# Eight rows of V sent for before the sixteenth row of U, a last V row moved from VectorE to TensorE, and a store that no longer waits, in a one-layer diffusion backbone with a PEER expert stage

## The reference, cut to what matters

```
q  = hx @ w_q                                  # per head two halves of 128
v1, i1 = top_k(q1 @ k1.T, 16); v2, i2 = top_k(q2 @ k2.T, 16)
score, pos = top_k(v1[:, None] + v2[None, :], 16);  idx = (i1 * 128 + i2)[pos]
gate = softmax(score)
act  = gelu(sum_d w_u[idx] * hx)               # 16 dot products of 2048
out += sum_k (gate * act)[k] * w_v[idx[k]]     # 16 rows of 2048
```

## Time and profile before

| | |
|---|---|
| median of 3 runs | 3055.89 us (3055.28 to 3056.6) |
| the profiled execution's own time | 3055.89 us |
| its span in the trace | 3054.1 us |
| PE, DVE, ACT, POOL busy | 87%, 63%, 30%, 20% of the span |
| DMA | 902.85 MB, 296 GB/s over the span |
| gathers of U and V | 256 and 256, of 1 MB each |

### The profile page before, as it was taken

The page is one execution under the profiler, slowest core; times in us unless marked ns, Lnnn a source line. Parts: engine busy times, 40 slices in busy tenths (PEclk is TensorE's granted clock), DMA queues, the critical chain, the costliest instruction groups (busy, mean ns, idle before and its releaser), DMA issues.

```text
span 3054.1 us, 31614 instructions
## 1 busy us (share of the span) xinstructions
PE 2652.6 (87%) x11033; PEld 1802.4 (59%) x11033; DVE 1931.8 (63%) x2623; ACT 911.5 (30%) x1240; POOL 607.3 (20%) x580
## 2 busy tenths in 40 slices
PE   8899997999998999999999956969778876868777
PEld 3488875878776879999878723434333432323332
DVE  1389997444555868888556675555555565656656
ACT  1067765442444333333444110101111111101100
POOL 0000000000000000000000174434344435443333
PEclk9999998999999999999999988989989998989999
DMA  8533333552422877888556699999999999999999
GB/s 337 220 124 124 110 109 127 193 190 85 152 83 112 337 307 304 334 339 316 193 207 237 247 420 409 422 421 412 421 412 421 403 422 411 421 403 421 421 422 376
DMA packets 126508, 902.85 MB, mean 296 GB/s; under 512 B 14016, under 2 KB 15552, under 8 KB 17216
## 3 DMA queue, kind: packets, MB, share of 16 engines
q0 software_dynamic: 82944, 604.02, 48.0%
q1 hardware_dynamic: 38736, 278.94, 24.4%
q10 hardware_dynamic: 4720, 18.57, 1.6%
HBM read 899.33 MB, written 2.13 MB: 295 GB/s over the span
## 4 chain that ended last, share of the span: by engine, by line
PE 44%; DMA 28%; DVE 13%; issue 9%; ACT 3%; POOL 2%; DVEq 0%; ACTq 0%; POOLq 0%
DMA u<-in_peer_u,idx 26%; PE ps L446 9%; PE ps L489 8%; PE ps L490 7%; PE ps L491 7%; PE ps L766 5%; PE ps L504 3%; DVE u L1671 2%; DVE wl L1149 2%; DMA v<-in_peer_v,idx 2%; POOL u L1756 1%; POOL v L1766 1%; ACT wh L828 1%; DVE ub L1233 1%; PE ps L643 1%
## 5 line engine op out<-in xcount | busy, mean ns | idle before, releaser
L766 PE MATMUL ps<-v,dg 128*128 128x512 f32 x1920 | 878.4, 614 | 178.0 <-DMA v<-in_peer_v,idx 101.8
L1671 DVE SCALAR_TENSOR_TENSOR u<-u,hN 128x2048 f32<-128x2048 f32 x256 | 586.4, 2291 | 470.8 <-DMA u<-in_peer_u,idx 459.6
L1149 DVE TENSOR_TENSOR wl<-w,wh 128x1024 fp32r<-128x1024 f32 x432 | 524.4, 1221 | 408.8 <-ACT wh L828 407.8
L766 PEld LDWEIGHTS ps<-v,dg 128*128 128x128 f32 x1920 | 368.3, 196 | 683.9 <-issue 512.4
L828 ACT ACTIVATE wh<-w 128x1024 fp32r<-128x1024 f32 x432 | 453.5, 1058 | 679.2 <-PE ps L491 411.9
L1756 POOL DMA_INDIRECT u<-in_peer_u,idx x256 | 279.3, 1091 | 846.1 <-DVE u L1671 447.3
L446 PE MATMUL ps<-both,wh 128*128 128x256 f32 x2048 | 372.3, 285 | 5.2 <-DVE y L1361 5.1
L1101 ACT ACTIVATE dg<-con,wt 128x128 f32<-128x128 f32 x240 | 93.1, 399 | 836.6 <-PE ps L766 832.1
L1766 POOL DMA_INDIRECT v<-in_peer_v,idx x256 | 293.9, 1148 | 175.0 <-PE ps L766 89.2
L446 PEld LDWEIGHTS ps<-both,wh 128*128 128x128 f32 x2048 | 320.9, 193 | 10.1 <-issue 8.9
L1748 POOL DMA_DIRECT2D mr<-in_wmod x64 | 34.0, 532 | 1399.6 <-DVE br_lo L1489 980.5
(11 more groups left out here) (240 smaller groups left out, 2803.4 us busy)
## 6 DMA issues: line engine op xcount, KB each, us to landing
w<-in_stream SPq DMA_DIRECT2D x260, 1024.0 KB, 4.8
mr<-in_wmod POOLq DMA_DIRECT2D x64, 1024.0 KB, 6.8
wg<-in_gates ACTq DMA_DIRECT2D x8, 512.0 KB, 3.5
wx<-in_stream SPq DMA_DIRECT2D x4, 1024.0 KB, 7.8
u<-in_peer_u,idx POOLq DMA_INDIRECT x256, 16.7
v<-in_peer_v,idx POOLq DMA_INDIRECT x256, 18.0
xs<-in_ctx ACTq DMA_DIRECT2D x1, 2048.0 KB, 17.2
xs<-in_x ACTq DMA_DIRECT2D x1, 2048.0 KB, 22.2
```

Of the source, the lines that this page charges most:

```text
L766: last = mm(ps[:, b, :], dg[:, k % 4, :], V[n % NV][:, b * 512:(b + 1) * 512], start=(k == 0), stop=(k == TOPK - 1))
L1149: tt(wl[p % SPLITS][:, :, :], W[s][:, q * PIECE:(q + 1) * PIECE, :], wh[p % SPLITS][:, :, :].bitcast(F32), ALU.subtract)\
L1671: stt(U[n % NU][:, :], U[n % NU][:, :], 1.0, hN[:, t, :], ALU.mult, ALU.mult, accum_out=dot[:, t, k:k + 1])\
```

## The change

Row 13 of the last tile goes from DVE to PE: DVE then has rows 1, 3, 5, 7, 9, 11, and PE the other ten. SP stores `out[0]` as soon as DVE has finished it, and no longer waits for the last gather to land. In head 0, POOL's order becomes: V rows 0 and 1 after U(0,0,3); the wait for two heads' queries and V rows 2 and 3 after U(0,0,6); the wait for four heads' queries and V rows 4 to 7 after U(0,0,12). The two loops behind are replaced by `turn(0, 0, begun=8)`: U(0,1,k) with V(0,0,k+8) for k below 8, U(0,1,k) alone for k from 8, and then the alternation of U(1,0,k) and V(0,1,k) as before.

```
-        ON_DVE = (1, 3, 5, 7, 9, 11, 13)
+        ON_DVE = (1, 3, 5, 7, 9, 11)
...
             sp.wait_ge(*VX.at(0, "o"))
-            sp.wait_ge(v_in[NV - 1], PH * (2 * TOPK // NV) * 16)
             sp.dma_start(out[0], acc[:, 0, :]).then_inc(stored, 16)
...
-            def turn(h, odd, more=True):
+            def turn(h, odd, more=True, begun=0):
                 for k in range(TOPK):
                     rows_u(h, odd, 1, k)
-                    rows_v(h, odd, 0, k)
+                    if k + begun < TOPK:
+                        rows_v(h, odd, 0, k + begun)
...
             for k in range(TOPK):
                 rows_u(0, 0, 0, k)
-                if k == NU + 5:
+                if k == NU - 1:
+                    rows_v(0, 0, 0, 0)
+                    rows_v(0, 0, 0, 1)
+                if k == NU + 2:
                     pool.wait_ge(piece_used, 2 * (WQ0 + 4))
-                if k == TOPK - 1:
+                    rows_v(0, 0, 0, 2)
+                    rows_v(0, 0, 0, 3)
+                if k == NU + 8:
                     pool.wait_ge(piece_used, 2 * (WQ0 + 8))
-                if k >= NU - 1 and (k - NU + 1) % 3 == 0:
-                    rows_v(0, 0, 0, (k - NU + 1) // 3)
-            for k in range(TOPK):
-                rows_u(0, 0, 1, k)
-                if k in (2, 4, 6):
-                    rows_v(0, 0, 0, 4 + k // 2)
-                if k >= NV:
-                    rows_v(0, 0, 0, k)
-            for k in range(TOPK):
-                rows_u(1, 1, 0, k)
-                rows_v(0, 0, 1, k)
+                    for kv in range(4, 8):
+                        rows_v(0, 0, 0, kv)
+            turn(0, 0, begun=8)
```

## The result

The changed kernel takes 3080.83 us in the median of four runs (3078.01 to 3081.86) against 3056.24 (3055.28 to 3059.53) for the kernel before: the ratio is 1.0077, with a 95% interval of 1.0059 to 1.0095, so 18 to 29 us slower. I had forecast 3071.6 with a range up to 3077. The direction was right; 15.7 us was the forecast and 24.6 the measurement.

A forecast was written before the change was run, and what follows sets the result against it. The prediction took full DMA engines to bound the expert stage. To 3055.89 us it added 11.3 for the wait, 2.5 for the store and 1.9 for row 13, 15.7 in all, giving 3071.6 us, range 3059 to 3077.

The forecast's parts named there:

- What bounds the kernel: Expert stage: DMA engines are full, gathers land in issue order every 2.485 us; time is bytes plus DMA idle time.
- V rows earlier gain 0: Head 0's start: at most 1.7 us of ramp to fill and no bytes saved, so the gain was counted as 0.
- The wait of V(0,0,8), 11.3 us: Head 0: POOL waits for PE's first row, 10.54 us to issue plus 5.7 to land; a stall of 11.3 us.
- Eight U alone ... I take 0 and keep 1.8 for the range: Tile 1 of head 0, k from 8: DVE's dots at 2.7 us against 2.485 might lose 1.8 us, hidden, so 0.
- 1.1 us of slack: Head 0, U gathers only: landing to landing four gathers later takes 8.8 us, within four times 2.485.
- Six U in a row ... no gap: Head 0, U 7 to 12 of tile 0: four gathers later lands after 8.8 us, so no gap and no cost.
- The store, 2.5 us: End: out[0]'s early store shares the full DMA engines, so everything landing after it is 2.5 us late.
- row 13, 1.9 us: Last tile: PE gains a row of 3.43 us, ending its part and the first bank's addition 1.9 us later.
- Is it caught up later? No: Behind the stall in head 0 the stage is full again and ends by its bytes, so nothing is regained.
- The rivals: Whole kernel: covered stall, 3060.3 us (0.11); faster, 3039.6 (0.05); further stalls, 3081 (0.05); partial stall, 3066 (0.05).
- The stall breeds others: Head changes: holes deepen as DVE comes in a worse order; one further 9.5 us stall gives 3081 us; chance 0.05.

The follow-up runs named there:

- v8_at_3: pool_order with V(0,0,8) and its successors begun beside U(0,1,3), not U(0,1,0), and five U alone at the end: 3067.35 us, 1.0034 of the kernel before.
- pool_order: The changed kernel with only POOL's new order in head 0, row 13 and SP's wait as before: 3076.22 us, 1.0058 of the kernel before.
- stall_spread: pool_order with V rows 9 to 15 spread over tile 1, one for every two U, the early wait kept: 3071.68 us, 1.0041 of the kernel before.
- eight_u: The kernel before with V rows 5 to 15 moved ahead, so U(0,1,8) to U(0,1,15) stand alone, without the early wait: 3060.44 us, ratio 1.0008.
- eight_u_routed: eight_u with DVE's routing of head 0's tile 1 done earlier, none among the eight U alone: 3057.35 us, 1.0002 of the kernel before.
- pool_order_routed: pool_order with DVE's routing of head 0's tile 1 done earlier, behind dots 1 to 7: 3073.50 us, 1.0060 of the kernel before.
- store_early: The kernel before with only SP's wait ahead of the store of out[0] taken out: 3058.44 us, ratio 1.0005.
- no_stall: pool_order with V rows 8 to 15 of tile 0 issued only beside U(0,1,8) to U(0,1,15), so no early wait: 3064.08 us, 1.0023 of the kernel before.
- row13_to_pe: The kernel before with only row 13 of the last tile moved from DVE to PE: 3058.46 us, ratio 1.0001.
- scores_later: The kernel before with PE's scores of head h + 2 done behind the eighth V row of tile 1, not ahead of its first: 3053.02 us, ratio 0.9987.

## Why the prediction was wrong, by its own steps

- **What bounds the kernel: right.** The gathers land in order of issue at 2.485 us each, and the stage costs its bytes plus idle time of the DMA engines.
- **V rows earlier gain 0: right.** Nothing in head 0 became faster.
- **The wait of V(0,0,8), 11.3 us: right in mechanism, a little small.** 12.1 in the trace, 12.8 and 13.1 in two other kernels. The chain up to the issue held (10.66 us against 10.54); the gather behind it took 6.4 us and not 5.7. v8_at_3 shows the same term from the other side.
- **"Eight U alone ... I take 0 and keep 1.8 for the range": this is the step that failed.** It cost 5.8 us after the change, 6.5 between pool_order and stall_spread, 4.9 in its own stretch of eight_u (last dot 5.6). Three things in it were wrong. I had spread DVE's routing evenly over the dots of a window, 0.41 us each; the pieces that fall behind dots 8 and 9 take 1.8 and 1.4 us, and they stand where no V gather is queued to fill in. The two weight loads that were to hide it were issued at 1875.36, when GB/s had been down to 46 at 1865. And the "1.1 us of slack" did not exist: landing to landing of four gathers later is 10.0 to 10.9 us in eleven pairs of dots without routing between them (in six kernels), and not 8.8. eight_u_routed and pool_order_routed show the place of the routing to be the larger part of the cause: in the run itself 3.2 of 4.9 us and 4.5 of 6.0 come back. The slack that was not there fits the rest, which no run takes away.
- **"Six U in a row ... no gap": wrong too, by about 2 us.** It rested on the same 8.8 us, and left out DVE's routing behind dots 4 to 6. The first loop made U(0,0,15) late by 3.9 us after the change, and by 2.0 to 3.5 in the five other kernels with this loop. Not all of that is the order's: the kernels with the old loop are 0.2 to 1.4 late there. The loss that only the new loop shows lies between the dots of U(0,0,10) and U(0,0,13), 2.4 us after the change and 1.1 to 2.8 in the five others, against at most 0.3 with the old loop; the hole at 1770 is part of it. No run isolates it.
- **The store, 2.5 us, and row 13, 1.9 us: right**, each alone (2.5 and 1.9) and together (4.3). The Trainium skill ("DMA: Bandwidth & Descriptors", "Issuing engines are not separate DMA queues") says that transfers started by different engines interleave on the same 16 DMA engines; store_early agrees, with 2.5 us for a store of 1 MB. The same page's fit ("Anatomy of one DMA") gives an estimate of 4.4 us for a lone DMA of 1 MB, and would have made the wait 10.0 us; the trace has 6.4 and 12.1, so here the fit is too short.
- **"Is it caught up later? No": right.** Heads 1 to 7 even added 3.3 us in the profiled execution. In pool_order they added 0.8, in no_stall they gave back 0.2, so this belongs to the one execution more than to the change. The windows of 2.5 us place it at the head changes: counted as bytes missing from 420 GB/s between U(1,0,5) and the last dot, the holes are worth 19.0 us there, 16.3 in pool_order, 14.9 before, and 12.1 in row13_to_pe, whose heads 1 to 7 gave back 2.2. Why one execution has deeper holes than another stays open.
- **The rivals.** None of them came. The measured 3080.8 us is nearly the 3081 of "The stall breeds others", to which I had given 0.05, but that is a coincidence: its stall was to come at the head changes, and it came in head 0, from DVE and from the U buffers.

The sum with what was measured: 3.9 + 12.1 + 0.4 + 5.8 + 4.4 = 26.6 in the profiled execution, without its 3.3 of heads 1 to 7; the medians are 24.6 apart, and I had 15.7.

## What to carry to other kernels

When a queue is kept full by two streams, one paced by an engine's consumption and one filling in, check any stretch in which the filler is missing with the pacer's slowest interval there, instruction by instruction, and not with its mean over a window. Take the time from one landing to the landing that it allows from two such rows, and not from a sum of least times: here the sum gave 8.8 us and the rows 10.1. A wait put at the front of an in-order issuer costs the producer's whole chain less what is already queued behind it: three more gathers ahead of the wait, with the rest of the order that goes with them, took 12 of 22 us away. And time the small edits by an event clock inside the trace (here the dots), over as short a stretch as holds the effect: behind the last dot, 1.9 and 2.5 us stood out from executions that agree within 0.2 us and were invisible in the ratio, while over the whole stage the same program differed by 3.4 us.

## What the runs showed of the hardware that I had not expected

A hole in GB/s is not always its worth in time. At their deepest the six holes at the head changes read 282 down to 111 GB/s in windows of 2.5 us, and all of them went in scores_later. Counted as bytes missing from 420 GB/s, the holes between U(1,0,5) and the last dot fell from 14.9 to 4.2 us, but the landings came only 2.5 us sooner and the median 4.5. After the wait in the changed kernel the two agreed: the windows from 1797.5 to 1817.5 miss 12.8 us of bytes, and the landings lost 12.1. In the first case the share never fell below 0.49, in the second it was zero for 7.5 us. GB/s and the share are means over 16 engines, while a gather counts as landed only when its semaphore has all its 16 steps. Engines that run ahead and are done early would look like this, and the low windows at 3010 to 3020 fit it, but no row here shows the single engines, so that stays a reading.
